# Column strips for the score matrices of two gated recurrences, and a dense tile cut in two between them

## The reference, cut to what matters

```
# GLA, one direction, chunk of 64
q_e = q * exp(b);  k_e = k * exp(-b)          # b: cumulative log decay in the chunk
scores = einsum('bhncd,bhnsd->bhncs', q_e, k_e);  scores = where(mask, scores, 0)
o_intra = einsum('bhncs,bhnse->bhnce', scores, v)

# HGRN2: S_t = diag(f_t) S_{t-1} + (1-f_t) i_t^T ; o_t = S_t^T q_t
f = lb + (1.0 - lb) * sigmoid(f_raw);  g = log(f);  k = 1.0 - f
decay = exp(b_t - b_s)  for s <= t             # b: cumulative g
a = einsum('bhtk,bhsk,bhtsk->bhts', qc, kc, decay)
o_intra = einsum('bhts,bhsv->bhtv', a, vc)
```

## Time and profile before

| | |
|---|---|
| median of 3 runs | 1459.5 us |
| profiled execution, its time | 1460.08 us |
| profiled execution, its span | 1458.3 us |
| mean granted TensorE clock | 0.977 of full speed |
| TensorE (matmuls) busy | 1385.7 us (95%) |
| VectorE busy | 761.8 us (52%) |
| ScalarE busy | 575.7 us (39%) |
| GpSimd busy | 556.3 us (38%) |
| TensorE weight loads busy | 1143.9 us (78%) |

### The profile page before, as it was taken

How to read it: one execution, slowest core, us unless ns; L and a number is a source line. 1 busy time by engine, 2 the same in 40 slices (tenths; PEclk the granted TensorE clock), 3 DMA queues, 4 the chain that set the end, 5 groups by cost and what they waited for, 6 DMA issues and landing times.

```text
span 1458.3 us, 18620 instructions
## 1 busy us (share of the span) xinstructions
PE 1385.7 (95%) x6812; PEld 1143.9 (78%) x6812; DVE 761.8 (52%) x1223; ACT 575.7 (39%) x777; POOL 556.3 (38%) x126
## 2 busy tenths in 40 slices
PE   7899999998997999999999799997999999999997
PEld 4688888876885888888888577766888888887886
DVE  3641451655737878877521352235777777302453
ACT  6443453442334222223222445554445554334233
POOL 4232323323343434433434233224444455434341
PEclk8999999998998999999999999998999999999998
DMA  6122212223323445545333242322222211232221
GB/s 189 55 87 87 80 50 74 85 73 116 115 87 100 131 131 154 147 130 152 96 99 98 59 130 86 101 58 58 58 58 58 58 58 58 61 113 86 87 87 58
DMA packets 201599, 133.68 MB, mean 92 GB/s; under 512 B 3479, under 2 KB 197768, under 8 KB 201558
## 3 DMA queue, kind: packets, MB, share of 16 engines
q1 hardware_dynamic: 200390, 130.68, 30.5%
q10 hardware_dynamic: 848, 1.60, 0.3%
q0 software_dynamic: 320, 0.84, 0.2%
HBM read 130.99 MB, written 2.12 MB: 91 GB/s over the span
## 4 chain that ended last, share of the span: by engine, by line
issue 68%; POOL 15%; PE 14%; ACT 1%; DMA 1%; POOLq 0%; SPq 0%; ACTq 0%; DVE 0%
POOL wlo L426 15%; PE acc L441 4%; PE acc L443 3%; PE acc L442 3%; PE acc L1723 1%; DMA raw<-in_w_in_dram 1%; PE acc L1725 1%; PE acc L1724 1%; PE mid L2091 0%; ACT hhi L669 0%; PE mid L2150 0%; ACT whi L422 0%; POOLq L1696 0%; SPq L528 0%; POOL masks L1690 0%
## 5 line engine op out<-in xcount | busy, mean ns | idle before, releaser
L426 POOL TENSOR_TENSOR wlo<-raw,whi 128x2048 fp32r<-128x2048 f32 (+2 forms) x112 | 550.0, 4911 | 873.3 <-ACT whi L422 873.3
L441 PE MATMUL acc<-hhi,whi 128*128 128x512 f32 x1152 | 461.5, 401 | 18.0 <-POOL wlo L426 15.9
L442 PE MATMUL acc<-hlo,whi 128*128 128x512 f32 x1152 | 450.9, 391 | 0.0
L443 PE MATMUL acc<-hhi,wlo 128*128 128x512 f32 x1152 | 450.6, 391 | 0.0
L441 PEld LDWEIGHTS acc<-hhi,whi 128*128 128x128 f32 x1152 | 217.6, 189 | 71.2 <-POOL wlo L426 19.7
L442 PEld LDWEIGHTS acc<-hlo,whi 128*128 128x128 f32 x1152 | 217.7, 189 | 46.0 <-issue 2.9
L443 PEld LDWEIGHTS acc<-hhi,wlo 128*128 128x128 f32 x1152 | 217.4, 189 | 46.4
L422 ACT ACTIVATE whi<-raw 128x2048 fp32r<-128x2048 f32 (+2 forms) x112 | 205.7, 1836 | 58.9 <-PE acc L443 42.7
L1388 DVE TENSOR_TENSOR ada<-ada 128x512 f32<-128x512 f32 x24 | 109.1, 4545 | 0.8
L441 PE MATMUL acc<-ahi,whi 128*128 128x512 f32 x176 | 68.7, 390 | 0.0
L442 PE MATMUL acc<-alo,whi 128*128 128x512 f32 x176 | 68.5, 389 | 0.0
(11 more groups left out here) (353 smaller groups left out, 2019.1 us busy)
## 6 DMA issues: line engine op xcount, KB each, us to landing
raw<-in_w_in_dram SPq DMA_DIRECT2D x57, 512.0 KB
raw<-in_w_in_dram SPq DMA_DIRECT2D x26, 1024.0 KB
raw<-in_w_ffn_in_dram SPq DMA_DIRECT2D x44, 512.0 KB
ada<-in_w_ada_dram SPq DMA_DIRECT2D x24, 512.0 KB, 3.8
raw<-in_w_ffn_out_dram SPq DMA_DIRECT2D x16, 704.0 KB
raw<-in_w_out_dram SPq DMA_DIRECT2D x8, 1024.0 KB
xnat<-in_x_dram SPq DMA_DIRECT2D x8, 512.0 KB, 7.0
raw<-in_w_branch_gla_dram SPq DMA_DIRECT2D x4, 1024.0 KB
```

Source lines behind the costliest of these rows:

```text
L426: nc.gpsimd.tensor_tensor(wlo[:, slot, 0:n], raw[:, slot, 0:n], whi[:, slot, 0:n].bitcast(f32), ALU.subtract).then_inc(s_unit_lo, 1)
L441: nc.tensor.matmul(acc[bank][:, :], h, xh[:, k, :], start=(k == 0), stop=False)
L442: nc.tensor.matmul(acc[bank][:, :], h, xl[:, k, :], start=False, stop=False)
L443: last = nc.tensor.matmul(acc[bank][:, :], lo, xh[:, k, :], start=False, stop=(k == nk - 1))
```

## The change

1. `hg_scores` no longer holds the levels; they move to `hg_levels(g, first, end)`, and the key-value products to `hg_kv(g)`. The order on TensorE becomes: tile 2, transposes, levels 0 to 3, first half of tile 3 (12 matmuls, `pe_part`), levels 4 to 7, key-value products, second half of tile 3, `hg_out`.
2. A level no longer multiplies whole blocks of 128 tokens. For level 0 and the levels whose stretch is at most 32 tokens (1 to 5), each block is cut in four strips of 32 tokens: weights of 32 columns, moving columns of the same strip (32 for level 0, 16 for the others), output on the 32 PSUM partitions of the strip. Level 6 takes two products of 32 x 32 in each block, level 7 one of 64 x 64: left half as weights, right half as moving columns.
3. In `gla_scores` each full product becomes its two diagonal quarters of 64 x 64.

The masks and everything on the other engines stay as they were.

```diff
@@ gla_scores
                     for t in range(TT):
-                        ts = slice(t * P, (t + 1) * P)
-                        mm(M[2 + d][:, ts], ke[:, d, ts], qe[:, d, ts], start=True, stop=True)
+                        for c in range(2):
+                            cs = slice(t * P + c * CHUNK, t * P + (c + 1) * CHUNK)
+                            mm(M[2 + d][c * CHUNK:(c + 1) * CHUNK, cs], ke[:, d, cs], qe[:, d, cs], start=True,
+                               stop=True, skip_group_check=True)
@@
+            def score_strips(n):
+
+                half = 1 << max(n - 1, 0)
+                if 2 * half <= STRIP:
+                    blocks = [slice(c, c + STRIP) for c in range(0, P, STRIP)]
+                    return [(b, b, b) for b in blocks]
+                return [(slice(c, c + half), slice(c, c + half), slice(c + half, c + 2 * half))
+                        for c in range(0, P, 2 * half)]
@@ hg_scores
                 last.then_inc(s_h_ktr, 1)
-                for n in range(LEVELS + 1):
+
+            def hg_levels(g, first, end):
+                for n in range(first, end):
...
                     for t in range(TT):
-                        ts = slice(t * P, (t + 1) * P)
-                        if n == 0:
-                            last = mm(M[2][:, ts], hk[:, ts], hq[:, ts], start=True, stop=True)
-                        else:
-                            last = mm(right_halves(M[(n + 2) % 4][:, ts], n - 1), hw[:, n - 1, ts],
-                                      right_halves(hw[:, n - 1, ts], n - 1), start=True, stop=True)
+                        for rows, left, right in score_strips(n):
+                            ls = slice(t * P + left.start, t * P + left.stop)
+                            rs = slice(t * P + right.start, t * P + right.stop)
+                            if n == 0:
+                                last = mm(M[2][rows, rs], hk[:, ls], hq[:, rs], start=True, stop=True,
+                                          skip_group_check=True)
+                            elif right == left:
+                                last = mm(right_halves(M[(n + 2) % 4][rows, rs], n - 1), hw[:, n - 1, ls],
+                                          right_halves(hw[:, n - 1, rs], n - 1), start=True, stop=True,
+                                          skip_group_check=True)
+                            else:
+                                last = mm(M[(n + 2) % 4][rows, rs], hw[:, n - 1, ls], hw[:, n - 1, rs], start=True,
+                                          stop=True, skip_group_check=True)
                     last.then_inc(s_h_score, 1)
+
+            def hg_kv(g):
                 pe.wait_ge(s_h_mask, g * 9 + 7)
@@ hg_iteration
                 hg_scores(g)
-                tile(base, 3, 1, 1, 4, h)
+                hg_levels(g, 0, 4)
+                b, _, free = TL(base, 3, 4, h)
+                pe.wait_ge(s_acc_free[b], free)
+                pe_part(b, 1, 1, 0, KT // 2)
+                hg_levels(g, 4, LEVELS + 1)
+                hg_kv(g)
+                pe_part(b, 1, 1, KT // 2, KT)
                 hg_out(g)
```

More of the change, by code:

```diff
@@ L29 @@
 BW = 640
+STRIP = 32
 C_Q, C_K, C_V, C_R = 0, 512, 1024, 2048
```

## The result

The changed kernel takes 1461.7 us at the median (1460.5 to 1467.2, 20 runs) against 1458.0 us (1456.3 to 1460.0, 20 runs) for the kernel before: a ratio of 1.003 with a 95% interval of 1.0022 to 1.0037. The forecast was 1462. So the change cost 3.7 us, although TensorE now gets through the scores of a head in less than half the time (3.3 us for the eight levels, where it was 7.1).

A forecast was written before the change was run, and what follows sets the result against it. Bound: a loop through TensorE, VectorE and GpSimd, almost level with TensorE's own work. Profiled 1460.1 - 7.3 (loop) - 3.8 (last head) + 13.7 (low clock) + 0 (GLA) = 1462.7, or 1462 against the median; range 1447 to 1481.

The forecast's parts named there:

- Strips: HGRN2 score levels on TensorE: 11 ns a record, bounds 7 and 31; levels 0 to 3 end at 1.5 us.
- The rival in which strips don't run side by side: HGRN2 score levels: a record costs 31 ns, the loop grows 2.8 us a head, 1493 us in all; chance 0.11.
- The loop: HGRN2 cycle of scores, masks, states, VectorE run, GpSimd, tile 2: 1.0 to 1.05 us shorter a head, -7.3 us.
- The gate of q: VectorE step behind masks and states in each HGRN2 head: 8.05 us behind level 0, against 9.08 before.
- GpSimd's turn: GpSimd's `wlo` ahead of tile 2: gets through only after VectorE's 14.5 us run, then takes 4.5 us.
- TensorE's saving: `hg_out` starts 3.8 us earlier a head; kept only at the last head, -3.8; elsewhere the gap becomes 4.0 us.
- The clock: Tile 2 behind the longer gaps: 1.2 GHz in all seven heads, mean 1.95 us lost each, +13.7 us, range 0 to +21.
- The rival in which the clock stays up: Gaps ahead of tile 2: no low clock follows, so some 1448 us against the median; chance 0.20.
- GLA: GLA scores in four heads: 0.8 us saved each goes into longer waits for `kf`, about 6 us; net 0.
- The chances: Odds for the whole kernel's time: faster 0.32, same 0.27, slower 0.41, with 0.2% as the border of same.

The follow-up runs named there:

- e4: The changed kernel with twelve unused matmuls between tile 1 and tile 2 of seven heads, filling TensorE's gap: 1448.5 us, ratio 0.9926 to the kernel before.
- e1: The kernel before with strips in the HGRN2 scores alone, tile 3 uncut and GLA as before: 1440.6 us, ratio 0.988.
- e5: e1 plus a VectorE wait for GpSimd's `wlo` ahead of its run over `hw`: 1427.8 us, ratio 0.979 to the kernel before.
- e7: e1 plus a VectorE copy of one PSUM element ahead of hkd*hk in heads after the first: 1431.2 us, ratio 0.9819 to the kernel before.
- e3: The kernel before with only the GLA scores cut into diagonal quarters: 1459.6 us, ratio 1.0006.
- e8: e5 with ScalarE's copies moved ahead of its whi split: 1423.1 us, ratio 0.9756 to the kernel before.

## Why the prediction was right

**Strips.** Forecast 11 ns a record with bounds of 7 and 31. Level 0 took 8 (32 records in 0.27 us), next to the low bound; with the pauses between levels, levels 0 to 3 took 12 (128 records), and ended at 1.54 us (forecast 1.5). The rival in which strips don't run side by side is out. The Trainium skill's floor of about 25 ns from start to start ("TensorE: Matmul & The Clock Gate", under the gap of 56 ns) does not hold for strips: the trace has 8 ns. That page's section on packing small matmuls, with strips that start some 4 ns apart, comes nearer.

**The loop.** The gate of q came at 8.27 us (forecast 8.05), and the low clock removed (e4) the seven periods got shorter by 6.3 us (forecast 7.3). The missing 1.0 is this 0.2 us a head, and it arose ahead of level 4, which started at 4.50 (forecast 4.25): the half tile took 2.96 us (1044.13 to 1047.09) where 2.75 had been counted. From there to the gate, 3.77 against 3.80, the schedule was right. e1, e5 and e7 are the proof that this loop sets the period: to bring the gate forward by 2.57 us shortened six periods by 2.5 each, and to take GpSimd's turn out of it shortened them by another 1.5.

**TensorE's saving.** `hg_out` came at 9.78 (forecast 9.5), and the saving stayed at the last head alone: -4.0, forecast -3.8. In the others it became gap: 3.7 to 3.9 us a head (forecast 4.0), 27.0 in all.

**The clock.** Forecast: low behind all seven gaps, 1.95 us each, +13.7. Measured: all seven, +13.7 by e4 (13 to 15 by the medians and ratios). The mechanism was right, but that the sum agrees to the tenth is luck: the single costs are of two sizes, 1.5 and 2.6, which the forecast didn't foresee, and four of one and three of the other happen to have the mean of the four stretches it was taken from. The rival in which the clock stays up gave 1448; e4 is that kernel in effect, and took 1448.5.

**GLA.** Forecast 0, measured 1.0006 in e3. The wait for `kf` grew to 6.1 us as forecast (about 6).

The sum of what was measured, -6.3 - 4.0 + 13.7 = +3.4, stands against +2.6 in the forecast, and the medians differ by 3.7. The sum was close because the term for the loop was off by 1.0 and the others by 0.2 or less. The time itself, 1461.7 against 1462, agrees better than the difference does, and that is luck too: the forecast started from a median of 1459.5, which 20 runs put at 1458.0, and so the start was 1.5 too high and the rise 1.1 too low. Whether the change counts as the same or as slower hung on less than a microsecond: 0.2% above 1458.0 is 1460.9. The chances (0.27 and 0.41) reflect that. What the forecast did not look for is the better use of the same insight: with the turn of GpSimd named as the hinge, the way to win was to move that turn, not TensorE's work.

## What to carry to other kernels

When TensorE waits for a loop that runs through other engines, a faster TensorE makes the gap wider, and a gap of a few microseconds can cost more than it looks, if the clock behind it is low (1.5 to 2.6 us for each gap here): the strips and the cut brought TensorE forward by 3.5 us a head, and the time got longer. Follow the loop to the step that nothing can overlap, and change that: one wait of VectorE ahead of its long run saved 13 us, 9 of them inside the loop. Cutting a dense tile to hide a chain of masks is worth doing only if the piece put in front is not itself ahead of what the loop waits for.

## What the runs showed of the hardware

- Products with 32-column weights on four places go at 8 ns a record, rounds of four in 32 ns; with 64-column weights on two places at about 30 ns (GLA: 32 records, 0.98 us to the next start); with 128 columns at 111. The count of records rose from 64 to 216 a head and their time fell from 7.1 to 3.3 us.
- The clock fell to 1.2 GHz at each of the seven gaps of 3.7 to 3.9 us ahead of tile 2, and at none of the gaps of 1.1 to 1.3 us in the same place (the kernel before, e1, e4); the low stretches lasted 3.4 and 6.8 us in turn. This is not a rule on the length of one gap: in the first head of e8 the clock fell during a wait of 1.4 us, which followed waits of 0.3 and 0.4 us among the narrow matmuls.
- A GpSimd operation that reads SBUF is not served while VectorE goes through products of two SBUF operands without a break (11.7 us in place of 4.56), and it gets in at VectorE's next read of a PSUM bank, be it of one element. It then holds VectorE's next such product to its own end (5.03 us in place of 0.69). The Trainium skill says in "SBUF — State Buffer", Who interferes with whom, that whichever has the shared pair of ports keeps it for the whole instruction, and that issue order decides who blocks. The trace agrees, and adds that an operation that is already waiting does not get in between two products issued back to back.
